# Moving three SBUF regions of a one-core mLSTM layer down by 384 bytes

## The reference

```
u = rmsnorm(x, mix_norm_g)
q, k, v, o_pre, if_pre = split(u @ w_in)            # 8 heads, q and k of 64, v of 128
h = mlstm over chunks (matrix memory, stabilised by a running maximum)
y = (rms(h) * norm_g * sigmoid(o_pre)) @ w_out
h = x + y
out = h + (silu(rmsnorm(h, ffn_norm_g) @ w_gate) * (rmsnorm(h) @ w_up)) @ w_down   # d_ff 2816
```

## Time and profile before

| | |
|---|---|
| median of 3 runs | 2225.83 us (2224.99 to 2229.47) |
| profiled execution | 2225.83 us |
| its span, first to last instruction | 2224.2 us |
| TensorE matmul busy | 2142.0 us, 96% |
| VectorE busy | 1458.7 us, 66% |
| ScalarE busy | 924.0 us, 42% |
| GpSimd busy | 282.8 us, 13% |
| mean granted TensorE clock | 0.985 |
| moved by DMA | 281.56 MB, 127 GB/s |

### The profile page before, as it was taken

One profiled execution on the slowest core, in us unless ns is written; L12 is line 12 of the kernel. 1 busy time (PEld: TensorE's weight loads), 2 busy tenths in 40 slices (PEclk: granted clock), 3 DMA queues, 4 the chain that ended last, 5 costly groups with the idle time before them and its releaser, 6 DMA issues.

```text
span 2224.2 us, 29465 instructions
## 1 busy us (share of the span) xinstructions
PE 2142.0 (96%) x10424; PEld 1778.0 (80%) x10440; DVE 1458.7 (66%) x2274; ACT 924.0 (42%) x1670; POOL 282.8 (13%) x373
## 2 busy tenths in 40 slices
PE   6999989989999999999989999799899999999999
PEld 4788868878888888788878888688688888888887
DVE  8765467686757565579677644667866665656774
ACT  4443653344333333345434346433433333333443
POOL 4111111120101010100112111111210010101000
PEclk8999999999999999999999999899999999999999
DMA  4333354213232324864514334532033323257433
GB/s 143 100 114 109 106 217 143 86 48 114 100 113 92 110 96 137 295 225 115 151 62 131 98 104 151 208 119 91 32 116 103 101 96 116 94 192 248 151 122 115
DMA packets 200288, 281.56 MB, mean 127 GB/s; under 512 B 12912, under 2 KB 131696, under 8 KB 200176
## 3 DMA queue, kind: packets, MB, share of 16 engines
q1 hardware_dynamic: 171696, 183.07, 26.1%
q0 software_dynamic: 28480, 97.02, 12.5%
HBM read 197.73 MB, written 82.31 MB: 126 GB/s over the span
## 4 chain that ended last, share of the span: by engine, by line
PE 86%; DVE 6%; DMA 3%; issue 2%; ACT 1%; SPq 1%; POOL 0%; DVEq 0%; ACTq 0%; POOLq 0%
PE ps L2163 12%; PE ps L2166 12%; PE ps L2165 12%; PE ps L1912 7%; PE ps L1916 7%; PE ps L1914 7%; PE ps L2209 6%; PE ps L2213 5%; PE ps L2211 5%; PE ps L1825 2%; PE ps L1827 2%; PE ps L1826 2%; PE ps L1832 1%; DMA vtc<-proj_hbm 1%; DMA g_in<-ops_hbm 1%
## 5 line engine op out<-in xcount | busy, mean ns | idle before, releaser
L1666 DVE TENSOR_TENSOR ring<-raw_f,ring 128x512 fp32r<-128x512 f32 x308 | 211.5, 688 | 188.1 <-ACT ring L1103 186.7
L1103 ACT CAST ring<-raw_f 128x512 fp32r<-128x512 f32 x308 | 190.9, 623 | 212.4 <-PE ps L2166 198.4
L2163 PE MATMUL ps<-u_lo,ring 128*128 128x512 f32 x704 | 275.3, 391 | 0.0
L2166 PE MATMUL ps<-u_hi,ring 128*128 128x512 f32 x704 | 274.1, 389 | 0.0
L2165 PE MATMUL ps<-u_hi,ring 128*128 128x512 f32 x704 | 274.0, 389 | 0.0
L2209 PE MATMUL ps<-ring,ring 128*128 128x512 f32 x616 | 241.3, 392 | 6.3 <-DVE ring L1744 6.3
L2213 PE MATMUL ps<-ring,ring 128*128 128x512 f32 x616 | 240.4, 390 | 0.0
L2211 PE MATMUL ps<-ring,ring 128*128 128x512 f32 x616 | 240.3, 390 | 0.0
L2163 PE MATMUL ps<-t_op,ring 128*128 128x512 f32 x528 | 207.5, 393 | 6.2 <-DVE ring L1666 6.2
L2165 PE MATMUL ps<-t_op,ring 128*128 128x512 f32 x528 | 207.1, 392 | 0.0
L2166 PE MATMUL ps<-t_op,ring 128*128 128x512 f32 x528 | 206.9, 392 | 0.0
(11 more groups left out here) (219 smaller groups left out, 4253.8 us busy)
## 6 DMA issues: line engine op xcount, KB each, us to landing
ops_hbm<-kept POOLq DMA_DIRECT2D x154, 256.0 KB, 2.4
g_in<-ops_hbm SPq DMA_DIRECT2D x154, 256.0 KB, 2.7
raw<-in_ml_w_in_dram SPq DMA_DIRECT2D x24, 1024.0 KB, 5.4
proj_hbm<-pkept POOLq DMA_DIRECT2D x96, 256.0 KB, 2.7
raw_f<-in_ffn_w_gate_dram SPq DMA_DIRECT2D x44, 512.0 KB, 4.7
raw_f<-in_ffn_w_up_dram SPq DMA_DIRECT2D x44, 512.0 KB, 4.7
b<-in_ffn_w_down_dram SPq DMA_DIRECT2D x88, 256.0 KB, 4.9
x_in<-in_x_dram SPq DMA_DIRECT2D x16, 512.0 KB, 6.0
```

The source lines that it names most:

```text
L1103: nc.scalar.copy(four(ring[slot][:, 0, :]), feed_source(q, s)).then_inc(w_hi_done, 1)
L1666: nc.vector.tensor_tensor(four(ring[slot][:, 1, :]), feed_source(q, s), four(ring[slot][:, 0, :].bitcast(F32)), ALU.subtract).then_inc(w_l ...
L2163: pe.matmul(banks(bank), wh, moved(kind, 1, k), start=(fresh and k == 0), stop=False, skip_group_check=True)
L2166: last = pe.matmul(banks(bank), wl, moved(kind, 0, k), start=False, stop=(k == 3), skip_group_check=True)
```

## The change

The pad at the end of `r_q` becomes P = 128 bytes in place of 512, in the size of the region and in the start of the third `hg` buffer. That buffer moves down by 384 bytes within `r_q`, and everything that is allocated after `r_q` (`r_a`, `r_b`, `r_c` and the small tiles) moves down by 384 bytes. Nothing in `r_u`, in `r_v` or in the rest of `r_q` moves. The new starts are 147,968 (`r_a`), 164,352 (`r_b`) and 180,736 (`r_c`), all three multiples of 512. The third `hg` buffer starts on a multiple of 512 as well. No instruction, transfer, wait or order is added, removed or moved.

```
-        r_q = region(32 * KB + 512)
+        r_q = region(32 * KB + P)
...
-        hg_at = [r_q, r_q + 8 * KB, r_q + 24 * KB + 512]
+        hg_at = [r_q, r_q + 8 * KB, r_q + 24 * KB + P]
```

## The result

The changed kernel takes 2248.3 us (median of 4 runs, 2246.48 to 2250.45) against 2225.74 us for the kernel before. The ratio is 1.0098, with a 95% interval from 1.0081 to 1.0116 (the two medians alone give 1.0101). The forecast was no change, with a range up to 2229.5 us. The instructions, their order and their operands' shapes are the same on every engine; only addresses differ.

What follows compares the result with a forecast made beforehand. The prediction took TensorE's matmuls, 86% of the chain, to bound the kernel. It added 0 for matmuls, 0 for VectorE and ScalarE and 0 for transfers to 2225.83 us, giving 2225.8 us, range 2221.5 to 2229.5 us.

Steps and rivals of the forecast that it cites:

- What bounds the kernel: Whole span: TensorE busy for 2142.0 of 2224.2 us, 86% of the chain; only 11.4 us in reach of transfers' speed.
- 0.43 ns for each matmul: Over 10,424 matmuls, the change in each that makes 4.5 us, the 0.2% a measurement can tell from no change.
- Matmuls: 0: TensorE's matmuls: no change, since lines 2163 and 2209 differ in place and region yet both have medians of 389 ns.
- VectorE and ScalarE: 0: Their instructions on the chain, 133 us: no change, with 0.9 us to each side.
- Transfers: Loads and stores of moved tiles: 0 taken; bounds were 7.0 us gained or 8.0 us lost at four waits.
- 2 us and a queue share lower by a tenth: Sign for a transfer gain: a `vtc` wait of 2 us and that lower share in the crowded stretches.
- the rival in which a part of the fee goes: Loads into moved regions lose a 128-byte first piece per row: 3.6 us less, 2222.2 us; chance 0.09.
- The sum: Whole kernel: 2225.83 us plus 0 for matmuls, 0 for VectorE and ScalarE, 0 for transfers, giving 2225.8 us.
- Two operands fall into each other's way: DVE splits with ring slot and source newly 384 bytes apart: DVE's chain part 5% longer, 2232.5 us; chance 0.06.
- The unequal distance that was held against it: DVE split with `b` from `r_u` and ring in `r_q`, 256 bytes unequal, has the lowest median, 685 ns.

Runs made afterwards that it cites:

- the run of pairs: Layer left out, only groups of 48 matmuls of 128x512 at small distances and mixed pairings; plain float32 took 41.4 us at a distance of 0 as of 128.

## Why the prediction was wrong, point by point

**What bounds the kernel** was right: TensorE, with the long product stages at 100%. So was the remark that 0.43 ns for each matmul would be 4.5 us. The matmuls are where the time went, 27.3 us / 10,424 = 2.6 ns each on average.

**Matmuls: 0 was wrong, and it is the step that failed.** I compared line 2163 with line 2209 and took from their equal 389 ns that places don't matter. The two differ in their absolute places, 128 and 384 past a multiple of 512, but not in what counts: both have operands a multiple of 256 bytes apart, as have all 128x512 matmuls in float32r in the kernel before. The trace of before does not hold one such matmul of the other kind, so it could not bound the cost. I wrote "I have no row that gives another bound", and went on as if the bound were zero. What the runs showed in place of the 0 is 27.3 us more of TensorE's time, 4,616 matmuls at 5.9 ns, with the distance as the cause: the same move by 256 bytes costs nothing, and all tiles moved together cost nothing. I also asked whether the distance between two tiles that are read together could matter, and weighed it for VectorE alone, where it costs nothing: the tile pair inside TensorE's own stream, weights and moving operand, was not named. The one reader with truly odd rows, `v1` at steps of 516 bytes, is of products in plain float32, which the run of pairs shows unslowed at 32, 64 and 128 bytes, so it would hardly have warned me (steps of 4 were not tried in it).

**VectorE and ScalarE: 0 was right.** The medians of lines 1666 and 1738 are within 1 ns of before, and the busy times of the two engines within 0.7 and 1.2 us.

**Transfers.** A value of 0 for place was about right. From 303 to 317.5 us the changed kernel's queue 1 reads

```profile
q1 hardware_dynamic: 1673, 4.37, 79.8%
```

which is 110.7 ns for 2,612 bytes, against 110.2 ns for 2,649 in the earlier trace rows before. The `vtc` waits are 3.3 us each, and the prediction had asked for 2 us and a queue share lower by a tenth before it would believe in a gain; neither came. What a start on 256 gives was seen in the runs that move all tiles: at most 0.24%, the size of the rival in which a part of the fee goes (2222.2 us). That is a chance agreement, for that rival has the loads become shorter, and it was the stores out of SBUF that did. Of the 4.3 us that the changed kernel gives back, 3.2 us are the waits at `g_in` that are gone. They are no gain of the transfers' place: with all tiles up by 128, `g_in` starts on a multiple of 256 too, and the two waits are still 1.8 and 2.1 us. The sum had no term for it, that a slower TensorE hides a late transfer.

**The rivals.** "Two operands fall into each other's way" was the right kind of mechanism, a new distance of 384 bytes between two streams, with the right sign. That is luck in part: it was put on the wrong engine and priced on 6% of the chain in place of 86%. Its chance of 0.06 followed from that. The unequal distance that was held against it, 256 bytes, costs matmuls nothing either, so it said nothing of 384.

## What to carry to other kernels

Where two float32r operands of a matmul are placed by hand, keep weights and moving operand a multiple of 256 bytes apart: any other distance that was tried alone costs 1 to 4.4% of the time from one 128x512 matmul to the next, and the profile shows no wait for it, only a mean duration of 391 to 399 in place of 389 ns. In the layer a line mixes fast and slow matmuls: that of `t_op` in line 2163 keeps its median of 389 ns in the changed kernel, and its mean is what moves. So compare the mean and median of a matmul with the best one of the same shape before asking what it waits for. And a trace in which a property never varies says nothing about that property: look for the pair that differs before taking a zero from two equal rows.

## What the runs showed of the hardware that was not expected

- float32r, 128x512: starts 227 ns apart at distances of 256 and 512 bytes, 229 at 64 and 320, 232 to 234 at 8, 16, 24, 32, 96, 128 and 160 to 224, 237 at 4. bf16 (starts 216 ns apart, 0 to 512 bytes) and plain float32 (41.4 us for 96 records, 0 to 128 bytes) are the same at every distance tried.
- The Trainium skill's page "SBUF — State Buffer", section "A bandwidth-pool intuition that's wrong (but worth ruling out)", gives TensorE an independent second read port for weights, in a row on bf16. For bf16 no run speaks against it. For float32r the places of the two operands are not independent: with nothing else running, 48 matmuls take 11.4 us in place of 11.0 at a distance of 128 bytes.
- A float32r unit with an even distance behind one with an odd distance is slow in its first matmuls, 230.9 ns in place of 226.7 over a unit of 12.
- The transfers of GpSimd's queue, most of them stores out of SBUF, took 12.5% of the DMA engines' span with tiles 128 bytes past a multiple of 256, and 11.3% with tiles on one.
